# Two attentions and an mLSTM on one core: turned items copied before the next exponential, the first item inside the last dense block, the first decay weights beside the drain, heads' values one item later

## The chip, the cores and the metric

The kernel runs on one core of a Trainium2 chip. The metric is device time in microseconds (us) of one launch on that core; lower is better. TensorE (PE) multiplies, VectorE (DVE) and ScalarE (ACT) work on rows of 128 partitions, GpSimd (POOL) adds sums of squares, SyncE (SP) issues the weight transfers.

## What is computed

The reference runs two transformer blocks over one sequence of 512 tokens, width 1024, fp32. The change touches only the middle of the first block. Cut to that:

```python
h = rms_norm(x, mix_norm_pre)
(nq, kc, vc, ksl, vsl, kwn, vwn, gt, mq, mk, mv, mi, mf, mo) = split(h @ w_in)
o = native_sparse_attention(...)      # 8 heads of 64, compressed + selected + window branches, gated
hm = mlstm_chunkwise(mq, mk, mv, ...) # 4 heads, weights decay with distance, causal
y = concatenate([y_nsa, sigmoid(mo) * hm]) @ w_out
x = x + rms_norm(y, mix_norm_post)

h = rms_norm(x, xattn_norm_pre)
q = h @ w_xq;  k, v = split(rms_norm(mem) @ w_xkv)   # 4 heads of 256, 256 memory tokens
p = softmax(q k^T);  o = p v
x = x + rms_norm(o @ w_xo, xattn_norm_post)
```

Behind it come SwiGLU layers, a conformer convolution and a stick-breaking attention, which the change leaves as they are.

## The kernel before

Everything lives in SBUF; weights stream through a ring of four slots of 512 KB. A dense product splits weight and operand into a high and a low fp32r part and makes three products of them (`unit`, whose matmuls are all recorded at L515): one unit is 8 chunks x 3 products x 2 halves, 48 matmuls of 256 columns, and fills one PSUM bank. ACT makes the high part of each weight slot (`w_hi`, L1305), DVE the low part (`w_lo`, L1803). Each engine has its own program, written out by hand; they are held together by counting semaphores, so the order of the statements in each engine's loops is the order in which its instructions run. There are eight PSUM banks.

**The sparse attention** walks over 32 items, `NSA_ITEMS` = 4 column groups `c` x 4 query blocks `qb` x 2 branches. An item is 128 queries, two heads at once ("half"), and 128(qb+1) keys. Its steps:

1. PE: scores (`nsa_scores`, L854), into banks 0/1 or 2/3 by the item's parity; it waits until DVE has added item s-2.
2. DVE: adds the bias and finds the row maximum (`nsa_add`, L2159, two instructions).
3. ACT: exponential with row sum (L1466, two instructions).
4. DVE: reciprocal and scale (`nsa_scale`, L2166 and L2169).
5. PE: transposes the scaled item, "turns" it, into banks 4 and 5 (`nsa_turn`, L866). There is one pair of these banks, so it waits until ACT has copied the item before.
6. ACT: copies the turned item to `pT` (L1475).
7. PE: multiplies it with the values into bank 6 or 7 (`nsa_values`, L882); every eighth item adds the compressed branch (L888), and ACT and DVE take `h_hi` (L1483) and `h_lo` (L2149) out.

PE's round s does scores(s), turn(s-3), values(s-4). ACT's round s does exp(s), then copy(s-3). DVE's round s does add(s), scale(s-1). At items 8, 9, 16 and 17 (`NSA_SPLITS`) ACT and DVE also split one weight slot for the product with `w_out`. The first items stand behind the last `w_in` block, number 13, whose result DVE takes out (L1823); `in_values` transposes mLSTM values (L712) that DVE copies to `v_ml` (L1945), and `cmp_values_in` makes `v_cmp` (L2007, L2012).

**The mLSTM** follows: 8 items, each with scores (`ml_scores`, L902), decay weights by ACT (`ml_decays`, L1443/L1445), a product of the two by DVE (`ml_weight`, L2192), values (`ml_values`, L916), then column sums of one column each (L928, L935) and factors (L946).

**The cross attention** has 16 items, 4 heads x 4 query blocks, against 256 memory tokens: scores (L1051, banks 0 and 1), row maximum by DVE (L2310), exponential by ACT (L1532), reciprocal and scale by DVE (L2315, L2316), turn (L1061, banks 2 and 3), copy by ACT (L1542, two instructions of 128 columns), and after a head's fourth item its values (L1071, 8 slow matmuls in the trace's count), whose result ACT and DVE take out as `h_hi` (L1547) and `h_lo` (L2323). Then the product with `w_xo` follows (`dense_then_halves`).

## Time and profile before

| | |
|---|---|
| median of 3 runs | 2852.51 us (2851.51 to 2855.64) |
| the profiled execution's own time | 2848.28 us |
| its span in the trace | 2846.5 us |
| PE busy | 2768.2 us, 97% |
| DVE, ACT, POOL busy | 51%, 38%, 9% |

The profiled execution is 4.23 us below the median of the runs. PE is busy 97% of the span; the few places where it isn't are what a change of order can touch. A busy PE in this profile can still be a PE at half its clock.

### The profile page before, as it was taken

To read this page: it belongs to the slowest core of one execution; us is meant where nothing else is said; L and a number is where in the kernel's file an instruction comes from. 1 tells how busy PE (TensorE), PEld (TensorE's weight loads), DVE (VectorE), ACT (ScalarE), POOL (GpSimd) and SP (SyncE) were. 2 spreads that over 40 slices of the span, in tenths; PEclk is the share of its full clock that TensorE was granted. 3 is DMA by queue.
4 is the path that set the end of the run, shared out by engine and by line. 5 is a ranking of instruction groups with operands and counts; after the bars stand their busy time and mean duration, and the time that the engine had idled before them with its cause. 6 is when DMAs were issued, how large, how long until landed. Compare 5 with 4: busy or idle time off the path is not lost.

```text
span 2846.5 us, 56267 instructions
## 1 busy us (share of the span) xinstructions
PE 2768.2 (97%) x23426; PEld 2635.6 (93%) x23426; DVE 1454.3 (51%) x1911; ACT 1079.2 (38%) x1597; POOL 246.9 (9%) x211
## 2 busy tenths in 40 slices
PE   7988998999999999999999999999999999999997
PEld 7965996999999999997799999999999986999997
DVE  6766563554424544347865443335444367544433
ACT  4456433532324323236653232224343246422321
POOL 2000200100000000006810000000000000100000
PEclk9999999999999999999999999999999999999999
DMA  5310231223232332331122323343323332223232
GB/s 201 111 53 16 88 128 38 82 96 103 86 102 80 104 103 87 95 101 67 38 68 96 103 89 100 94 147 106 102 88 96 104 130 86 67 96 101 89 95 71
DMA packets 75161, 263.96 MB, mean 93 GB/s; under 512 B 8388, under 2 KB 8516, under 8 KB 74752
## 3 DMA queue, kind: packets, MB, share of 16 engines
q1 hardware_dynamic: 69408, 248.93, 27.0%
q10 hardware_dynamic: 4608, 8.39, 0.8%
q0 software_dynamic: 992, 4.42, 0.5%
q8 instruction: 118, 1.93, 0.3%
q14 instruction: 35, 0.29, 0.0%
HBM read 253.29 MB, written 8.42 MB: 92 GB/s over the span
## 4 chain that ended last, share of the span: by engine, by line
PE 92%; DVE 4%; ACT 2%; issue 2%; DMA 0%; SPq 0%; POOLq 0%; POOL 0%; DVEq 0%; ACTq 0%
PE bank L515 80%; PE bank L1089 2%; PE bank L568 1%; PE bank L632 1%; PE bank L1229 1%; DVE w_lo L1803 1%; PE bank L1071 1%; PE bank L1249 1%; PE bank L1261 0%; PE bank L866 0%; ACT w_hi L1305 0%; DVE n_p L2159 0%; ACT n_p L1466 0%; PE bank L916 0%; PE bank L854 0%
## 5 line engine op out<-in xcount | busy, mean ns | idle before, releaser
L515 PE MATMUL bank<-h_hi,w_hi 128*128 128x256 f32 x4720 | 931.2, 279 | 1.0 <-DVE w_lo L1803 0.7
L515 PE MATMUL bank<-h_hi,w_lo 128*128 128x256 f32 x4720 | 922.5, 277 | 0.0
L515 PE MATMUL bank<-h_lo,w_hi 128*128 128x256 f32 x4720 | 921.9, 277 | 0.0
L1803 DVE TENSOR_TENSOR w_lo<-w_raw,w_hi 128x1024 fp32r<-128x1024 f32 x468 | 577.3, 1237 | 376.0 <-ACT w_hi L1305 202.1
L515 PEld LDWEIGHTS bank<-h_hi,w_hi 128*128 128x128 f32 x4720 | 714.9, 188 | 11.7 <-issue 8.1
L515 PEld LDWEIGHTS bank<-h_hi,w_lo 128*128 128x128 f32 x4720 | 713.6, 188 | 0.0
L515 PEld LDWEIGHTS bank<-h_lo,w_hi 128*128 128x128 f32 x4720 | 713.0, 188 | 0.0
L1305 ACT ACTIVATE w_hi<-w_raw 128x1024 fp32r<-128x1024 f32 x468 | 476.9, 1050 | 230.2 <-PE bank L515 162.4
L1823 DVE TENSOR_TENSOR t<-bank,rB 128x512 f32<-128x512 f32 x260 | 179.2, 690 | 510.0 <-PE bank L515 507.1
L515 PE MATMUL bank<-a_hi,w_hi 128*128 128x256 f32 x1716 | 334.2, 276 | 0.0
L515 PE MATMUL bank<-a_lo,w_hi 128*128 128x256 f32 x1716 | 334.0, 276 | 0.0
L515 PE MATMUL bank<-a_hi,w_lo 128*128 128x256 f32 x1716 | 334.0, 276 | 0.0
L1345 ACT ACTIVATE a_hi<-t 128x512 f32 (+1 forms) x110 | 69.6, 632 | 581.2 <-DVE t L1861 581.2
L515 PEld LDWEIGHTS bank<-a_hi,w_hi 128*128 128x128 f32 x1716 | 258.4, 188 | 0.0
L515 PEld LDWEIGHTS bank<-a_lo,w_hi 128*128 128x128 f32 x1716 | 258.2, 188 | 0.0
L515 PEld LDWEIGHTS bank<-a_hi,w_lo 128*128 128x128 f32 x1716 | 258.2, 188 | 0.0
L2535 POOL TENSOR_TENSOR acc<-acc,sq 128x512 f32<-128x512 f32 (+1 forms) x72 | 94.6, 1314 | 1702.8 <-ACT sq L1311 1700.5
L1311 ACT ACTIVATE sq<-x 128x512 f32<-128x512 f32 (+1 forms) x56 | 35.3, 631 | 339.5 <-DVE x L1870 304.5
L1343 ACT ACTIVATE t<-t 128x512 f32<-128x512 f32 x110 | 69.7, 634 | 187.7 <-DVE t L1823 187.5
L1863 DVE TENSOR_TENSOR a_lo<-t,a_hi 128x512 f32 (+1 forms) x110 | 76.2, 693 | 100.6 <-ACT a_hi L1345 100.6
L1812 DVE SCALAR_TENSOR_TENSOR h_lo<-x,vec,h_hi 128x512 fp32r<-128x512 f32 (+1 forms) x64 | 71.0, 1125 | 66.5 <-ACT h_hi L1313 66.5
L2585 POOL TENSOR_TENSOR c_acc<-c_acc,c_product 128x512 f32<-128x512 f32 x63 | 87.9, 1395 | 9.8 <-ACT c_product L1622 5.0
(327 smaller groups left out, 2556.3 us busy)
## 6 DMA issues: line engine op xcount, KB each, us to landing
w_raw<-in_w_gu SPq DMA_DIRECT2D x220, 512.0 KB, 3.3
w_raw<-in_w_dn SPq DMA_DIRECT2D x80, 512.0 KB, 3.6
w_raw<-in_w_dn SPq DMA_DIRECT2D x40, 384.0 KB, 3.1
w_raw<-in_w_pw SPq DMA_DIRECT2D x24, 512.0 KB, 3.3
w_raw<-in_w_in SPq DMA_DIRECT2D x22, 512.0 KB, 4.5
w_raw<-in_w_xkv SPq DMA_DIRECT2D x16, 512.0 KB, 3.3
w_raw<-in_w_kv SPq DMA_DIRECT2D x16, 512.0 KB, 3.2
stick_qkv<-t ACTq DMA_DIRECT2D x24, 256.0 KB, 2.0
```

The costliest lines, as they stand in the source:

```text
L515: last = nc.tensor.matmul(dst[:, c:c + HALF], w, o[:, at + c:at + c + HALF], start=start and c == 0, stop=stop, skip_group_check=True)
L1089: last = nc.tensor.matmul(bank[4 + c % 2][:], diag_w[:, at:at + P], conv_tap(c, k), start=k == 0, stop=k == n - 1)
L1305: nc.scalar.activation(cut(w_hi, slot, UNIT), cut(w_raw, slot, UNIT), ACT.Copy).then_inc(w_hi_made, 1)
L1311: nc.scalar.activation(sq[:, (k % 2) * S:(k % 2) * S + n], cut(src, c, n), ACT.Square).then_inc(squared, 1)
L1343: nc.scalar.activation(t0[:], t0[:], ACT.Silu).then_inc(acted, 1)
L1345: nc.scalar.activation(cut(a_hi, c), t1[:], ACT.Copy).then_inc(f_hi, 1)
L1803: V.tensor_tensor(cut(w_lo, slot, UNIT), cut(w_raw, slot, UNIT), cut(w_hi, slot, UNIT).bitcast(f32), sub).then_inc(w_lo_made, 1)
L1812: V.scalar_tensor_tensor(cut(lo, c, n), cut(src, c, n), col(gain, c), hi_c, mult, sub).then_inc(op_lo, 1)
L1823: return V.tensor_tensor(dst, src, r, mult)
L1863: V.tensor_tensor(cut(a_lo, c), t1[:], cut(a_hi, c).bitcast(f32), sub).then_inc(f_lo, 1)
L2535: G.tensor_tensor(acc[:, 0:n], acc[:, 0:n], sq[:, (c % 2) * S:(c % 2) * S + n], add).then_inc(summed, 1)
L2585: G.tensor_tensor(acc_c, cut(c_product, (n - 1) % 4) if i == 1 else acc_c, cut(c_product, n % 4), add).then_inc(c_product_used, 2 if i == ...
```

## The change

- Sparse attention. `nsa_scores(0)` moves into the middle of dense unit 13 (after four of its eight chunks), and DVE does `cmp_values_in`, `nsa_add(0)` and `nsa_scale(0)` before it takes that unit's result out. `nsa_turn(0)` comes right behind `in_values(4)`, which gets bank 7 of its own.
- ACT copies the turned item s-3 first and does the exponential of item s after it.
- DVE splits its weight slots one item later.
- mLSTM: the first two score products move up among the last sparse items, ACT does the first three decays in its rounds 32, 33 and 34 (between the last copies), DVE does `ml_weight(0)`, `ml_weight(1)` and `ml_add(1)` before the last `h_lo`. The values go to banks 4 and 5 instead of 6 and 7, so they wait for the last copy of a turned item, not for the last `h_lo`.
- Cross attention: the first scores wait for six of eight `xq` results instead of all; turns come three items behind the scores instead of two (`px` has four slots instead of three); ACT copies first and with one instruction of 2x128 columns instead of two; a head's values come one item later; the last head's values stand inside the first two units of the product with `w_xo`.

```diff
-ML_COLUMN_BANK, FACTOR_BANK = [4, 5], [5, 4, 6, 7]
+ML_COLUMN_BANK, FACTOR_BANK = [6, 7], [7, 6, 4, 5]
...
+                    unit(r // RING, r % RING, in_bank(i), range(KC), h_hi, h_lo, True, True, made=R0["mix"] if r == 0 else None,
+                         within=(lambda: nsa_scores(0)) if n == 13 else None)
...
-                    pe.wait_ge(v_stored, 5)
+                    pe.wait_ge(v_stored, 3)
...
-                    pe.wait_ge(op_lo, R0["nsa"] + 4)
+                    pe.wait_ge(n_pT, NI + 1)
...
-            for s in range(NI + 4):
+            in_values(4)
+            nsa_turn(0)
+            for s in range(1, NI + 4):
                 if s < NI:
                     nsa_scores(s)
-                if s < 2:
-                    in_values(4 + s)
-                if 0 <= s - 3 < NI:
+                elif s < NI + 2:
+                    ml_scores(s - NI)
+                if s == 1:
+                    in_values(5)
+                if 1 <= s - 3 < NI:
                     nsa_turn(s - 3)
                 if s >= 4:
                     nsa_values(s - 4)
-                if NI < s < NI + 3:
-                    ml_scores(s - NI - 1)
...
-            for s in range(16 + 2):
+            for s in range(16 + 3):
                 if s < 16:
...
+                    x_scores(s)
+                r = s - 3
+                if r == 0:
+                    pe.wait_ge(evacuated, BEND["xq"])
                 if r >= 0:
...
+                    x_turn(r)
+                    if r and r % TB == 0:
+                        x_values(r // TB - 1)
+
+            for j in range(2):
+                pe.wait_ge(w_lo_made, U0["xo"] + j + 1)
+            xo_chunks(0, range(4))
+            x_values(3)
+            xo_chunks(0, (4, 5))
+            xo_chunks(1, range(6))
+            for j in range(2):
+                xo_chunks(j, (6, 7)).then_inc(w_used, 1)
+            dense_then_halves("xo", h_hi, h_lo, "post_x")
...
-                if s == NI + 3:
-                    ml_decays(0)
+                if NI <= s < NI + 3:
+                    ml_decays(s - NI)
...
+                if n == 13:
+
+                    cmp_values_in()
+                    nsa_add(0)
+                    nsa_scale(0)
                 dve.wait_ge(w_used, r + 1)
...
+            turn_in_values(4)
+            for s in range(1, NI + 6):
+                if s < NI:
+                    nsa_add(s)
+                if s == 1:
+                    turn_in_values(5)
+                if 1 <= s - 1 < NI:
+                    nsa_scale(s - 1)
+                if s - 1 in NSA_SPLITS:
+                    split("out", 0, 4, NSA_SPLITS.index(s - 1))
+                if s == NI + 2:
+                    ml_weight(0)
+                if s == NI + 3:
+                    ml_weight(1)
+
+                    dve.wait_ge(n_turned, NI - 1)
+                    ml_add(1)
```

What stands on PE behind the last `w_in` unit, before. L854 are scores of an item (`kS` and `kW` are its two branches' keys), L712 is `in_values`, L866 a turn of the item in `n_p`:

```order
L515 MATMUL bank0<-h_lo,w_hi 128x256 x2
L854 MATMUL bank0<-kS,qT 128x128 [waits evacuated] x2
L712 MATMUL bank1<-cst,t0 128x128 [waits v_stored,v_ready]
L712 MATMUL bank1<-cst,t0 128x128 x3
L854 MATMUL bank0<-kW,qT 128x128 [waits evacuated] x2
L712 MATMUL bank1<-cst,t1 128x128 [waits v_stored,v_ready]
L712 MATMUL bank1<-cst,t1 128x128 x3
L854 MATMUL bank0<-kS,qT 128x256 [waits nsa_add] x2
L854 MATMUL bank0<-kW,qT 128x256 [waits nsa_add] x2
L866 MATMUL bank1<-cst,n_p 128x128 [waits v_stored,nsa_scaled,cmp_out,nsa_pT]
L866 MATMUL bank1<-cst,n_p 128x128 [waits nsa_scaled]
L854 MATMUL bank0<-kS,qT 128x384 [waits nsa_add] x2
```

and of the change, from the same place (L516, L762, L715 and L871 are the same statements):

```order
L516 MATMUL bank0<-h_lo,w_hi 128x256 x2
L715 MATMUL bank1<-cst,t0 128x128 [waits ml_colout,v_stored,v_ready]
L715 MATMUL bank1<-cst,t0 128x128 x3
L871 MATMUL bank1<-cst,n_p 128x128 [waits v_stored,nsa_scaled,cmp_out,nsa_pT]
L871 MATMUL bank1<-cst,n_p 128x128 [waits nsa_scaled]
L762 MATMUL bank0<-kW,qT 128x128 [waits evacuated] x2
L715 MATMUL bank1<-cst,t1 128x128 [waits v_stored,v_ready]
L715 MATMUL bank1<-cst,t1 128x128 x3
L762 MATMUL bank0<-kS,qT 128x256 [waits nsa_add] x2
L762 MATMUL bank0<-kW,qT 128x256 [waits nsa_add] x2
L762 MATMUL bank0<-kS,qT 128x384 [waits nsa_add] x2
```

The turn of item 0 stood behind four score products and both `in_values`; now it stands behind one `in_values`, and item 0's scores are gone from here, up into unit 13.

What stands on ACT for the last items, before. L1466 is an exponential (x2: both halves), L1475 the copy of a turned item, L1443 and L1445 the decays, L1483 `h_hi`:

```order
L1466 ACTIVATE n_p,small<-n_p,small 128x512 [waits nsa_add] x2
L1475 ACTIVATE pT<-bank1 128x2x256 [waits nsa_pv,nsa_turned]
L1466 ACTIVATE n_p,small<-n_p,small 128x512 [waits nsa_add] x2
L1475 ACTIVATE pT<-bank1 128x2x384 [waits nsa_pv,nsa_turned] x2
L1475 ACTIVATE pT<-bank1 128x1024 [waits nsa_pv,nsa_turned] x2
L1443 ACTIVATE decay<-ml_space,ml_col 128x128 [waits ml_masked,ml_stab_in,ml_colout]
L1445 ACTIVATE decay<-ml_space,ml_col 128x384
```

and of the change (L1512 exponential, L1507 copy, L1481 and L1483 decays, L1521 `h_hi`):

```order
L1507 ACTIVATE pT<-bank1 128x2x256 [waits nsa_pv,nsa_turned]
L1512 ACTIVATE n_p,small<-n_p,small 128x512 [waits nsa_add] x2
L1507 ACTIVATE pT<-bank1 128x2x384 [waits nsa_pv,nsa_turned]
L1512 ACTIVATE n_p,small<-n_p,small 128x512 [waits nsa_add] x2
L1507 ACTIVATE pT<-bank1 128x2x384 [waits nsa_pv,nsa_turned]
L1481 ACTIVATE decay<-ml_space,ml_col 128x128 [waits ml_masked,ml_stab_in,ml_colout]
L1483 ACTIVATE decay<-ml_space,ml_col 128x384
L1481 ACTIVATE decay<-ml_space,ml_col 128x128
L1483 ACTIVATE decay<-ml_space,ml_col 128x384
L1507 ACTIVATE pT<-bank1 128x1024 [waits nsa_pv,nsa_turned]
```

The first copy of 2x384 columns, item 28's, stood behind the last exponential, item 31's; now it stands ahead of it. Four decay instructions now stand ahead of the copy of item 30.

What stands on PE at the end of the cross attention, before. L1061 is a turn, L1071 a head's values, L515 the first unit of the product with `w_xo`:

```order
L1061 MATMUL bank0<-cst,px 128x128 [waits x_pT,x_scaled]
L1061 MATMUL bank0<-cst,px 128x128
L1071 MATMUL bank1<-pxT,vx 128x512 [waits op_lo,x_pT]
L1071 MATMUL bank1<-pxT,vx 128x512
L1071 MATMUL bank1<-pxT,vx 128x512 [waits op_lo]
L1071 MATMUL bank1<-pxT,vx 128x512
L515 MATMUL bank0<-h_hi,w_hi 128x256 [waits op_lo,w_lo_made,evacuated]
```

and of the change, the last turn, the fourth chunk of unit 0, the last head's values and the fifth chunk (L1069 turn, L1080 values, L516 unit):

```order
L1069 MATMUL bank0<-cst,px 128x128 [waits x_pT,x_scaled]
L1069 MATMUL bank0<-cst,px 128x128
L516 MATMUL bank0<-h_hi,w_hi 128x256 [waits op_lo,w_lo_made]
...
L516 MATMUL bank0<-h_lo,w_hi 128x256 x2
L1080 MATMUL bank1<-pxT,vx 128x512 [waits op_lo,x_pT]
L1080 MATMUL bank1<-pxT,vx 128x512
L1080 MATMUL bank1<-pxT,vx 128x512 [waits op_lo]
L1080 MATMUL bank1<-pxT,vx 128x512
L516 MATMUL bank0<-h_hi,w_hi 128x256 [waits op_lo]
```

Half a unit of dense work now stands between the last turn and the values that need its copy.

## Rows read from the trace of the kernel before

**Rows 1.** The page: busy time by engine

```profile
PE 2768.2 (97%) x23426; PEld 2635.6 (93%) x23426; DVE 1454.3 (51%) x1911; ACT 1079.2 (38%) x1597; POOL 246.9 (9%) x211
```

**Rows 2.** Windows, both attentions whole: length, busy by engine, granted clock, DMA share, GB/s

```profile
165.95:265.94 99.99, 79.12 (x642) 46.84 (x641) 70.45 (x244) 66.44 (x179) 7.83 (x17) 0.97 0.10 33
442.22:484.43 42.21, 33.66 (x129) 20.50 (x129) 17.96 (x56) 18.59 (x71) 0.00 (x0) 1.00 0.00 0
```

**Rows 3.** PE's waits in the sparse attention: total, times, longest

```profile
PE bank L866 <- ACT pT L1475: 14.2, 15, 1.8
PE bank L866 <- DVE v_cmp L2012: 3.5, 1, 3.5
PE bank L916 <- DVE decay L2192: 2.6, 1, 2.6
```

**Rows 4.** Windows between the exponentials of items 7 and 15, 23 and 31, and behind

```profile
183.89:207.69 23.80, 18.38 (x159) 11.10 (x158) 18.06 (x60) 16.54 (x43) 3.63 (x8) 1.00 0.14 45
...
231.50:251.59 20.09, 18.21 (x159) 11.07 (x157) 14.66 (x58) 14.68 (x41) 0.00 (x0) 1.00 0.01 2
251.59:265.94 14.35, 10.55 (x105) 6.88 (x102) 4.63 (x12) 9.18 (x20) 0.00 (x0) 1.00 0.00 1
```

**Rows 5.** Timeline of one round, items 28 to 31: start, us, engine, line

```profile
249.70 1.13 PE L854 MATMUL bank<-kW,qT 64*128 64x512 f32 x4
251.27 0.87 PE L866 MATMUL bank<-cst,n_p 128*128 128x128 f32 x6 [0.44 <-ACT pT L1475]
251.59 0.72 ACT L1466 ACTIVATE n_p<-n_p,small 128x512 f32<-128x512 f32 x1 [0.38 <-DVE small L2159]
253.02 0.79 ACT L1475 ACTIVATE pT<-bank 128x768 f32<-128x768 f32 x1
253.86 0.88 PE L866 MATMUL bank<-cst,n_p 128*128 128x128 f32 x6 [1.13 <-ACT pT L1475]
```

**Rows 6.** Timeline of the start, items 0 to 4

```profile
172.05 1.13 DVE L2012 TENSOR_SCALAR v_cmp<-bank,of_group 128x128 f32<-128x128 f32 x4
173.28 0.66 PE L866 MATMUL bank<-cst,n_p 128*128 128x128 f32 x2 [3.49 <-DVE v_cmp L2012]
173.87 1.65 PE L854 MATMUL bank<-kS,qT 64*128 64x384 f32 x4
```

**Rows 7.** Windows of the start: DVE's stretch, and a stretch of low clock

```profile
166.06:183.15 17.09, 13.28 (x68) 6.37 (x68) 14.38 (x55) 9.13 (x32) 0.56 (x1) 0.80 0.18 63
173.00:179.00 6.00, 5.72 (x20) 2.60 (x20) 4.15 (x18) 2.95 (x11) 0.00 (x0) 0.50 0.01 3
```

**Rows 8.** Timeline at a split (item 8): ACT, DVE and PE

```profile
187.77 1.06 ACT L1305 ACTIVATE w_hi<-w_raw 128x1024 fp32r<-128x1024 f32 x1
188.86 1.23 DVE L1803 TENSOR_TENSOR w_lo<-w_raw,w_hi 128x1024 fp32r<-128x1024 f32 x1 [1.36 <-ACT w_hi L1305]
192.17 1.09 PE L866 MATMUL bank<-cst,n_p 128*128 128x128 f32 x8 [1.45 <-ACT pT L1475]
```

**Rows 9.** Timeline of ACT: first and last of the first item's four decays

```profile
260.58 0.39 ACT L1443 ACTIVATE decay<-ml_space,ml_col 128x128 f32<-128x128 f32 x1
261.67 0.60 ACT L1445 ACTIVATE decay<-ml_space,ml_col 128x384 f32<-128x384 f32 x1
```

**Rows 10.** PE's waits in the cross attention

```profile
PE bank L1071 <- ACT pxT L1542: 4.3, 4, 1.3
PE bank L1061 <- DVE px L2316: 3.2, 4, 1.5
PE bank L1051 <- DVE qx L1824: 0.8, 1, 0.8
```

**Rows 11.** Window from one head's values to the next head's

```profile
451.27:461.64 10.37, 8.42 (x32) 5.17 (x33) 4.40 (x14) 4.69 (x18) 0.00 (x0) 1.00 0.01 2
```

**Rows 12.** Critical chain: a head's values, and the first four units behind

```profile
481.29 3.70 PE bank L1071 x8
484.99 22.61 PE bank L515 x192
```

262 lines of the change are left out of this document (130 added, 132 removed).

## The prediction

> **What bounds the kernel now.** I read the page first, then the chain of waits over the whole span, then windows and the timeline where the change reaches. The page says PE is busy 97% of 2846.5 us [rows 1]: whatever the change gains must come out of PE's idle time, or out of time in which PE is busy at half its clock. The diff touches no stage outside two stretches. In the first, from the end of the last `w_in` unit to the first mLSTM values, PE is busy 79.12 of 99.99 us, in the second, the cross attention, 33.66 of 42.21 us [rows 2]. So 20.87 and 8.55 us are idle, 29.4 together. PE does no less work after the change, and everything behind it (the `w_out` product, `w_xo`, the layers) starts from results of these stretches, with weight transfers that use a tenth of the DMA engines there [rows 2]. I take it that each microsecond cut here comes off the end.
>
> The waits say what PE stood for. In the first stretch: 14.2 us in 15 waits for ACT's copy of a turned item, 3.5 us in one wait for `v_cmp` at the start, 2.6 us for the first decay weight [rows 3]; they make up 20.3 of the 20.87. In the second: 4.3 us before the four heads' values, 3.2 us before turns, 0.8 us for the last `qx` [rows 10].
>
> **The copy first.** Rows 5 show one round. Scores(31) end at 250.83; the exponential of item 31 starts at 251.59 on them, its two halves run until the copy of item 28 can start at 253.02; turn(29) starts at 253.86, 0.04 behind the copy's end, and PE stood 1.13 us. Turn(28), the only thing the copy truly needs, was over at 252.14. So ACT was held by an exponential that nobody needs for three rounds. Now the copy of item s-3 stands ahead of exponential s. Behind exponential(30) it could start at 252.2 and end at 253.0; PE has values(27) and the next scores in between, until about 252.7 here and later in a full round. The wait falls to 0.3 us or nothing.
>
> What limits a group of eight items then? PE's own work in it is 18.2 to 18.4 us. Between the exponentials of item 23 and item 31 (no split) it takes 20.09 us; between items 7 and 15, and again between 15 and 23 (23.81 us, the same in its rows), two weight slots are split, and it takes 23.80 [rows 4]. DVE is busy 18.06 of these with a split and 14.66 without, ACT 16.54 and 14.68: with a split DVE is as full as PE, and the two hand items to each other. So:
> - Two groups with splits: the floor is 18.4; I put 0.7 us on it for the handing over between two full engines, 19.1. Gain 2 x 4.7 = 9.4. A split costs ACT 1.06 and DVE 1.23 us, and the turn behind it waited 1.45 [rows 8]; DVE's part goes an item later, where no exponential waits for it.
> - The group without: floor 18.2, I take 18.6. Gain 1.5.
>
> **The start.** Before, DVE took out unit 13, then stored values, added items 0, 1 and 2, scaled, made `v_cmp` (1.13 us and a small reduction), and only then PE could turn item 0: an idle stretch of 3.49 us [rows 6]. Behind it PE worked at half clock: granted 0.50 from 173 to 179 us, that is 1.2 of 2.4 GHz, with 5.72 us busy, and the scores of 384 keys took 1.65 us [rows 6, 7]. What moves ahead of the unit's end has room there: the unit takes some 5.7 us of PE (four take 22.61 [rows 12]), DVE has little to do in it, and item 0 at 128 keys is small. Only its four score matmuls lengthen the unit, by what they took behind it. From 166.06 to the last add of the group, 183.15, DVE is busy 14.38 of 17.09 us: 2.7 idle, in waits for scores at half clock, and its busy part loses 1.4 us of `v_cmp` and some 1.2 us of item 0 [rows 6, 7]. Together 5.3; less 0.4 for the score matmuls and something for waits that stay, because the first rounds are a chain of small steps on three engines: gain 4.0 us until item 7. Bounds: nothing, if the chain stays as long; 6.4 us, if the 3.49 goes and with it the half clock (5.72 busy at 0.50 is 2.9 us too many).
>
> The Trainium skill, "TensorE: Matmul & The Clock Gate", Part 1, says the clock is throttled by default and busy time releases it, and that idle gaps between groups of matmuls make it swing. The trace agrees so far as the half clock from 173 us follows 3.49 us of idle [rows 6, 7]. If frequent small gaps did it too, the first rounds would stay slow, the start would gain 1 us instead of 4, and the sum below would be 21.5.
>
> **The drain.** From item 31's exponential to the first mLSTM values it is 14.35 us with 10.55 PE busy [rows 4]: the idle 3.8 are the 1.13 above and 2.6 for `ml_weight(0)`, which stood behind the last `h_lo`, behind `h_hi`, behind the last values. Now `ml_weight(0)` needs the first decays and scores, which are two rounds old. But the decays (four instructions, 260.58 to 262.27, 1.7 us [rows 9]) now stand before the copies of items 30 and 31. With scores(31) ending at t, turns and values of 0.8 to 1.0 us each, copies of 0.7 and 0.9, scores of 0.9 to 1.1 (about as in [rows 5, 8]): turn(28) to t+0.9, copy(28) 1.6, turn(29) 3.4, copy(29) 4.2, decays 5.9, turn(30) 6.1, copy(30) 7.1 (PE free at 6.9: 0.2 idle), second decays 8.6, turn(31) 8.1, copy(31) 9.5 (PE free at 9.1: 0.4 idle), last values with the compressed branch 11.5. Before it was 15.1. I take 3.0 of these 3.6. The new order has queued nothing else behind the decays: `h_hi` of the last group comes after them and feeds `h_lo`, needed only for the `w_out` product some 20 us on, and for the column sums, which now wait for it in place of the first values; they stand four value products later.
>
> **The cross attention.** Start: the first scores no longer wait for the last `qx`, gain 0.8 [rows 10]. One head takes 10.37 us from values to values, PE busy 8.42, of which the values are 3.70 [rows 11, 12]; four items' scores and turns are the rest, 1.18 each. The two idle pieces: 1.2 to 1.3 before the values, since they follow the turn at once and need its copy; 0.5 to 0.8 in the first round after them, since DVE and ACT stood through 3.70 us and `h_lo` then got in the way. The first goes (the copy has a round of 1.18 us, and takes 0.4). The second half stays: ACT now does `h_hi` (two of 0.6) between the copies of items two rounds later, and I work out 0.8 us of idle for the scores that need the next exponential. So 9.2 a head instead of 10.37, for the two whole heads 2.4. At the end: before, values(3) ended at 484.99 and two units behind it would end at 484.99 + 2 x 5.65 = 496.3 [rows 12]. After: first values at 451.0 (442.2, five items of 1.18, three scores more of some 0.87, 0.3 of waits) instead of 451.27 although two more items' scores and one more turn stand ahead of them (2.4 us of work done early); heads 9.2 apart; the third head's values end at 473.1; three turns 474.1; half a unit 476.9; values(3) 480.6; the other 12 chunks of the two units 8.5, 489.1. Gain 7.2 for the whole stretch; the last `h_hi`, `h_lo` (about 2.5 us) lie under 5.6 us of chunks. That leaves 1.35 of 8.55 us idle, which is tight; I take 6.6. Bounds: 0.8 and 8.55. `px` and the merged copy cost nothing: one copy of 256 columns instead of two of 128, on an ACT busy 18.59 of 42.21 us [rows 2].
>
> **The sum.** 4.0 + 9.4 + 1.5 + 3.0 + 6.6 = 24.5 us. The profiled execution's 2848.28 become 2823.8; the median of the runs lies 4.2 above it, so I forecast 2852.5 - 24.5 = 2828.0.
>
> **The rivals.**
> 1. *The forecast:* most of the idle goes. Gains of 17 to 32 us, 2820 to 2835.
> 2. *The waits change their place.* DVE and PE both need 18 us of each split group, and the first rounds are small steps. Were a split group to take 21 us instead of 19.1, the start gain 1 and the drain 1, and the heads' idle come back behind `h_hi`, x 3: 2 x 2.8 + 1 + 1 + 1 + 3 = 11.6, 2841. For it: busy DVE of 18.06 in 23.80 [rows 4]. Against: PE's waits name the copy 15 times and an add hardly ever [rows 3]. The clock belongs here: a stretch of 6 us at 0.50 costs 2.9 [rows 7], and one at a new place would take that from the gain.
> 3. *The change does not do what it says:* turns wait not for ACT's order but for turn, copy, turn as a chain. A turn of 768 columns and its copy take 0.88 + 0.79 [rows 5], PE has scores and values of 1.7 to 2.0 us beside them; only with equal times would all waits stay. Then only v_cmp, weights and the x start go: 3.5 + 2.6 + 0.8 = 6.9 less new waits: within 0.2%, 2847 to 2855.
> 4. *Slower.* ACT is strictly in order. The exponential of item s now waits for turn(s-3), which PE does after scores(s). If DVE then scales late and adds late, scores and turns come late: each of 28 rounds would grow by a turn and a copy less the slack, 1.7 us at 384 keys. It decides when exponential(s) ends later than DVE's scale slot, which stands behind add(s+1), one whole round of about 2.3 us after. Copy and exponential are 0.79 + 1.43 = 2.2 [rows 5]: nearly a round. Were it 0.5 us over in each of the 28 rounds, 14 us, the decays' 1.7 on the last copies with it, against 3.5 + 6.6 gained: +5 to +8, 2859. Against it: the scaled item is only needed by a turn two rounds later still.
>
> The skill, "PSUM — Partial Sum Buffer", section "Engine vs sequencer instructions", says that ScalarE's and VectorE's queues are strict FIFO; rows 5 agree (the copy stood 0.9 us behind the exponential with its own input ready). That rule is what both 1 and 4 hang on.
>
> **Chances.** 1: 0.72. 2: 0.17. 3: 0.07. 4: 0.04. Less than 0.2% (5.7 us) is about what a measurement of this kernel can't tell from no change. Faster 0.88, same 0.08, slower 0.04. Range: the floor is all idle and the half clock gone, 29.4 + 2.9 = 32.3, so 2820; the top is rival 2, 2842.
>
> **What would show it.** After: turn(0) within 1.5 us of the end of unit 13, no wait for `v_cmp`, granted clock 1.00 through the start; the exponentials of items 7, 15, 23 and 31 at distances of 19.1, 19.1 and 18.6 us; PE's waits for the copy of turned items 14.2 -> under 4 us; no wait for the first decay weight; waits before a head's values gone, some 0.8 us for scores instead. If instead PE waits for adds or scales of DVE in the split groups, rival 2; if the copies still end last, rival 3; if exponentials start behind copies and DVE waits for them, rival 4. Wrong by another way: an extra stretch at half clock in the mLSTM's one-column sums, which the trace has already and whose place may shift.

## The result, and the profile after

The changed kernel takes 2820.79 us (median of 4 runs, 2815.65 to 2824.83) against 2852.01 us for the kernel before (4 runs beside it, 2851.0 to 2855.64): a ratio of 0.9887, 95% interval 0.9869 to 0.9906. That is 31.2 us less. The forecast was 24.5 us less, 2828.0, in a range of 2820 to 2842. The median lies 0.8 us above the low end of that range, and two of its four runs (2815.65 and 2819.87) lie below it. The direction and the places were right, the sum was 6.7 us too small. The profiled execution took 2815.65 us, its span is 2813.9 instead of 2846.5 us, 32.6 less.

The page's first line of the kernel after, which answers to [rows 1]:

```profile
PE 2761.1 (98%) x23426; PEld 2633.6 (94%) x23426; DVE 1454.2 (52%) x1911; ACT 1076.9 (38%) x1581; POOL 247.3 (9%) x211
```

PE makes the same 23426 matmuls. ACT has 16 instructions fewer, the merged copies of the cross attention. Windows of the kernel after (start and end, length, then busy us by engine, granted clock, DMA share, GB/s): the sparse attention whole, its three groups of eight items, the drain, the 6 us that ran at 0.50 before, one head of the cross attention, from values to values, and two places of low clock in the mLSTM behind:

```profile
166.60:244.49 77.89, 75.52 (x641) 46.03 (x639) 68.36 (x231) 65.21 (x175) 7.82 (x17) 1.00 0.12 42
179.80:198.36 18.56, 18.21 (x157) 11.15 (x158) 17.87 (x60) 16.41 (x44) 3.62 (x8) 1.00 0.18 58
198.36:216.87 18.51, 18.12 (x157) 11.05 (x158) 17.81 (x60) 16.36 (x43) 3.64 (x8) 1.00 0.17 58
216.87:234.83 17.96, 17.70 (x154) 10.89 (x156) 14.54 (x58) 14.69 (x41) 0.00 (x0) 1.00 0.01 2
234.83:244.49 9.66, 9.19 (x90) 5.92 (x88) 5.82 (x11) 8.38 (x20) 0.00 (x0) 1.00 0.01 3
...
173.00:179.00 6.00, 6.00 (x44) 3.09 (x44) 5.89 (x22) 5.39 (x17) 0.00 (x0) 1.00 0.01 3
426.85:435.37 8.52, 8.17 (x33) 5.30 (x33) 4.49 (x15) 4.28 (x14) 0.00 (x0) 1.00 0.01 2
...
256.00:259.00 3.00, 3.00 (x6) 1.58 (x7) 2.23 (x7) 0.30 (x1) 0.00 (x0) 0.50 0.00 0
273.00:276.00 3.00, 3.00 (x17) 3.00 (x16) 0.20 (x1) 0.18 (x1) 0.00 (x0) 0.50 0.00 0
```

In the sparse attention PE was idle 20.87 of 99.99 us [rows 2] and is now idle 2.37 of 77.89. A group with two split slots went from 23.80 to 18.56 and 18.51, the one without from 20.09 to 17.96, the drain from 14.35 to 9.66 [rows 4], a head from 10.37 [rows 11] to 8.52. The start runs at full clock where it had 0.50 [rows 7].

PE's waits after, in the sparse attention and then in the cross attention (total us, times, longest; L871 is the turn, L1060 the scores, L1069 the turn of the cross attention):

```profile
PE bank L871 <- ACT pT L1507: 0.8, 3, 0.3
PE bank L715 <- DVE v_ml L1983: 0.4, 1, 0.4
PE bank L762 <- DVE small L2108: 0.2, 1, 0.2
...
PE bank L1060 <- ACT px L1579: 1.0, 3, 0.4
PE bank L1069 <- ACT pxT L1574: 0.3, 1, 0.3
```

Against [rows 3, 10]: the copy's 14.2 us in 15 waits are 0.8 in 3, the waits for `v_cmp` and for the first decay weight are gone, and of the cross attention's 4.3 + 3.2 + 0.8 us there remain 1.3, two of them the 0.35 before scores that the forecast named. In the sparse attention DVE ends a wait of PE only twice, 0.6 us in all, and PE's values wait once more for the copy, 0.2 us. DVE did not become the bound, although it is busy 17.87 of 18.56 us.

The timeline of the drain after, ACT's part and the first mLSTM values on PE (start, us, engine, line):

```profile
234.13 0.81 ACT L1507 ACTIVATE pT<-bank 128x768 f32<-128x768 f32 x1
...
234.83 0.71 ACT L1512 ACTIVATE n_p<-n_p,small 128x512 f32<-128x512 f32 x1
...
236.58 0.81 ACT L1507 ACTIVATE pT<-bank 128x768 f32<-128x768 f32 x1 [0.23 <-PE bank L871]
...
237.28 0.39 ACT L1481 ACTIVATE decay<-ml_space,ml_col 128x128 f32<-128x128 f32 x1
...
239.08 1.22 DVE L2219 SCALAR_TENSOR_TENSOR decay<-bank,decay 128x1024 f32<-128x1024 f32 x1 [1.50 <-ACT decay L1483]
...
239.25 1.02 ACT L1507 ACTIVATE pT<-bank 128x1024 f32<-128x1024 f32 x1 [0.28 <-PE bank L871]
...
240.33 1.09 PE L871 MATMUL bank<-cst,n_p 128*128 128x128 f32 x8 [0.31 <-ACT pT L1507]
...
244.49 0.70 PE L921 MATMUL bank<-decay,v_ml 128*128 128x512 f32 x1
```

The copy of item 28 starts at 234.13, ahead of item 31's exponential and as soon as its turn is over; before, it stood behind both halves of that exponential and started 0.9 us after its turn was over [rows 5]. The first decay weight is started at 239.08 and done at 240.30, 4.2 us before PE asks for it; the decays ahead of the copies cost PE two short waits, 0.31 us before turn(31) and 0.17 us before its values.

**Where the 32.6 us of the two profiles went.** Event times of the traces, the kernel before and the kernel after; "T" is the start of the product of `cmp_w` and `cmp_h` just ahead of unit 13 (159.48 and 160.00), the last thing on PE that both kernels have alike:

| stretch | before | after | gain | forecast |
|---|---|---|---|---|
| start: T to item 7's exponential | 24.41 | 19.80 | 4.6 | 4.0 |
| items 7 to 15, 15 to 23 | 23.80, 23.81 | 18.56, 18.51 | 10.5 | 9.4 |
| items 23 to 31 | 20.09 | 17.96 | 2.1 | 1.5 |
| drain: to the first mLSTM values | 14.35 | 9.66 | 4.7 | 3.0 |
| to the first scores of the cross attention, without the wait for `qx` | 176.28 | 173.17 | 3.1 | 0 |
| cross attention to the end of its first four `w_xo` units, that wait counted | 65.22 | 56.66 | 8.6 | 6.6 |
| up to T, and all layers behind | | | -1.0 | 0 |

These marks are ACT's, and the change moves ACT's exponentials against PE: item 31's starts 2.67 us behind the start of its scores where it was 1.89. PE's own marks, the starts of scores(7), (15), (23) and (31), give each part its own gain. The windows before, from T to the first mLSTM values:

```profile
159.48:181.99 22.51, 18.73 (x145) 12.42 (x144) 14.41 (x54) 7.97 (x28) 0.56 (x1) 0.85 0.13 48
181.99:205.53 23.54, 18.34 (x159) 11.06 (x157) 17.79 (x60) 16.33 (x44) 3.17 (x7) 1.00 0.14 46
205.53:229.33 23.80, 18.33 (x159) 11.05 (x157) 17.98 (x60) 16.47 (x44) 3.64 (x8) 1.00 0.14 45
229.33:249.70 20.37, 18.20 (x159) 11.05 (x157) 15.03 (x58) 14.97 (x42) 0.45 (x1) 1.00 0.01 2
249.70:265.94 16.24, 12.00 (x111) 7.50 (x109) 6.39 (x19) 10.70 (x25) 0.00 (x0) 1.00 0.00 1
```

and after:

```profile
160.00:176.84 16.84, 15.95 (x145) 11.63 (x144) 13.16 (x51) 7.58 (x28) 0.56 (x1) 1.00 0.18 64
176.84:195.30 18.46, 18.13 (x159) 11.06 (x157) 17.77 (x61) 16.76 (x44) 3.17 (x7) 1.00 0.18 58
195.30:213.80 18.50, 18.12 (x158) 11.05 (x156) 17.80 (x61) 16.34 (x44) 3.64 (x8) 1.00 0.17 58
213.80:232.16 18.36, 18.06 (x159) 11.06 (x157) 14.94 (x59) 14.69 (x42) 0.46 (x1) 1.00 0.00 1
232.16:244.49 12.33, 11.86 (x110) 7.49 (x108) 8.45 (x20) 10.72 (x25) 0.00 (x0) 1.00 0.01 4
```

By these the start gained 5.7 us (forecast 4.0), the two split groups 10.4 (9.4), the group without 2.0 (1.5) and the drain 3.9 (3.0).

### The profile page after: what moved, and what is told of

The parts are those of the page before. It is cut to its first block, busy times and chain, and to the rows that moved or that the text cites. A ratio compares the mean times of both kernels' runs of the same rounds, so it can differ in the third digit from the quotient of the medians.

```text
span 2813.9 us, 56255 instructions
## 1 busy us (share of the span) xinstructions
PE 2761.1 (98%) x23426; PEld 2633.6 (94%) x23426; DVE 1454.2 (52%) x1911; ACT 1076.9 (38%) x1581; POOL 247.3 (9%) x211
## 4 chain that ended last, share of the span: by engine, by line
PE 93%; DVE 3%; ACT 2%; issue 1%; DMA 0%; SPq 0%; POOLq 0%; POOL 0%; DVEq 0%; ACTq 0%
PE bank L516 81%; PE bank L1127 2%; PE bank L569 1%; PE bank L633 1%; PE bank L1267 1%; PE bank L762 1%; PE bank L1287 1%; PE bank L871 1%; PE bank L1299 0%; PE bank L1080 0%; PE bank L887 0%; DVE w_lo L1841 0%; PE bank L921 0%; PE bank L1060 0%; DMA cst<-in_consts 0%
## 5 line engine op out<-in xcount | busy, mean ns | idle before, releaser
L516 PE MATMUL bank<-h_hi,w_hi 128*128 128x256 f32 x4720 | 931.1, 279 | 1.1 <-DVE w_lo L1841 0.8
L516 PE MATMUL bank<-h_hi,w_lo 128*128 128x256 f32 x4720 | 922.2, 277 | 0.0
L516 PE MATMUL bank<-h_lo,w_hi 128*128 128x256 f32 x4720 | 921.9, 277 | 0.0
L516 PEld LDWEIGHTS bank<-h_hi,w_hi 128*128 128x128 f32 x4720 | 714.6, 188 | 11.9 <-issue 8.1
L516 PEld LDWEIGHTS bank<-h_hi,w_lo 128*128 128x128 f32 x4720 | 713.2, 188 | 0.0
L516 PEld LDWEIGHTS bank<-h_lo,w_hi 128*128 128x128 f32 x4720 | 712.8, 188 | 0.0
L516 PE MATMUL bank<-a_lo,w_hi 128*128 128x256 f32 x1716 | 334.2, 276 | 0.0
L516 PE MATMUL bank<-a_hi,w_hi 128*128 128x256 f32 x1716 | 334.1, 276 | 0.0
L516 PE MATMUL bank<-a_hi,w_lo 128*128 128x256 f32 x1716 | 334.0, 276 | 0.0
L516 PEld LDWEIGHTS bank<-a_lo,w_hi 128*128 128x128 f32 x1716 | 258.4, 188 | 0.0
L516 PEld LDWEIGHTS bank<-a_hi,w_hi 128*128 128x128 f32 x1716 | 258.3, 188 | 0.0
L516 PEld LDWEIGHTS bank<-a_hi,w_lo 128*128 128x128 f32 x1716 | 258.2, 188 | 0.0
```

What stands on the lines that cost most here:

```text
L516: last = nc.tensor.matmul(dst[:, c:c + HALF], w, o[:, at + c:at + c + HALF], start=start and c == 0, stop=stop, skip_group_check=True)
```

## The experiments

Ten kernels, in the order in which they ran. Two lengths are used throughout, since each lies between two events of one trace and the rest of the span doesn't touch it: **T to mLSTM**, from T above to the first mLSTM values (106.46 before, 84.49 after), and **the cross stretch**, from its first scores to the end of the first four `w_xo` units (64.44 and 56.66). Where a gain is given from medians, the runs of one kernel scatter by 2 to 9 us, and by 24 in the 19 runs of the kernel before that stood beside the first four experiments.

### The copy first, alone

In the kernel before, ACT's loop copies item s-3 ahead of exponential s, and nothing else changes:

```diff
             for s in range(NI + 5):
-                if s < NI:
-                    for half in range(2):
-                        act.wait_ge(n_add, 2 * s + half + 1)
...
                 r = s - 3
...
                     nc.scalar.activation(dst, banks[1][:, 0:2 * S].rearrange("p (h n) -> p h n", n=S)[:, :, 0:n], ACT.Copy).then_inc(n_pT, 1)
+                if s < NI:
+                    for half in range(2):
+                        act.wait_ge(n_add, 2 * s + half + 1)
...
```

> The kernel before with one edit: in the sparse attention's loop ACT copies the turned item s-3 first and does exponential s after it. Theory A (the exponential held the copy): most of the 14.2 us in 15 waits for the copy goes; items 7, 15, 23, 31 stand some 20, 20 and 18.6 us apart instead of 23.8, 23.8 and 20.1; the kernel gains 9 to 13 us (ratio 0.9955 to 0.997). Theory B (turn, copy, turn is the chain, or DVE binds): the waits stay or change to waits for scores and adds; it gains under 3 us.

Measured: 2838.64 us against 2853.57, ratio 0.9936 (0.9916 to 0.9956). A split group and the group without a split:

```profile
184.59:204.00 19.41, 18.44 (x161) 11.22 (x160) 17.22 (x57) 16.56 (x44) 3.58 (x8) 1.00 0.16 55
223.45:241.41 17.96, 17.55 (x152) 10.66 (x152) 14.54 (x58) 14.70 (x41) 0.00 (x0) 1.00 0.01 2
```

PE's waits for the copy fell from 14.2 us in 15 to 3.0 us in 8; those for `v_cmp` (3.5) and the decay (2.6) stayed. T to mLSTM is 94.53, 11.9 us less by one exchange in one loop. The median fell by 14.9 us, more than the 9 to 13 named; the 11.9 of the trace is within them. The group without a split has its whole gain by this; the split groups have 4.4 of their 5.3. That the copy stood behind an exponential that nobody needed yet is shown: nothing else was moved.

### The cross attention, alone

The kernel before with the cross attention of the change only: first scores ahead of the last `qx`, four `px`, one copy of both halves, turns a round later, values an item later, the last head's values inside the two first units.

```diff
-            for s in range(16 + 2):
+            for s in range(16 + 3):
...
-                r = s - 2
+                r = s - 3
...
+                    x_turn(r)
+                    if r and r % TB == 0:
+                        x_values(r // TB - 1)
...
+            xo_chunks(0, range(4))
+            x_values(3)
+            xo_chunks(0, (4, 5))
+            xo_chunks(1, range(6))
```

> The kernel before with the cross attention's part of the change alone (scores before the last qx, turns three items behind, copy first and in one instruction, values an item later, last head's values inside the first two units). Theory A (the two parts are independent): from the end of xq to the end of the first four xo units it takes the 56.7 us that the whole change shows, against 65.4 before, so 8.7 us less, and the kernel gains 8 to 9 us (ratio 0.997). Theory B (part of that gain comes from the earlier stretches or from the clock): under 6 us.

Measured: 2842.62 us, ratio 0.9955 (0.9936 to 0.9975). The cross stretch is 56.68, the same as in the whole change, so the two parts of the change don't act on one another. The profiled T to mLSTM was 108.15 here, 1.7 more than in the kernel before with the same instructions: items 15 to 23 took 25.40 us at a granted clock of 0.93, not 23.81 at 1.00. That was the first sign that the half clock has its own part in these lengths.

### Without the start

The changed kernel with the start of before: item 0's scores not in unit 13, `v_cmp` and `in_values` back behind it.

```diff
-                         within=(lambda: nsa_scores(0)) if n == 13 else None)
...
-            in_values(4)
-            nsa_turn(0)
-            for s in range(1, NI + 4):
+            for s in range(NI + 4):
```

> The changed kernel with the start put back: item 0's scores, add and scale and v_cmp behind the last w_in unit, turn(0) in round 3. Theory A: PE idles 3 to 3.5 us before turn(0) again and falls to half clock behind it; 6 to 7 us slower than the changed kernel (item 7's exponential again 17 to 18 us behind the unit's end). Theory B (the copy order alone would have shortened the start): 3 us or less slower.

Measured: 2825.35 us, ratio 0.9893 (0.9854 to 0.9931), 4.6 above the changed kernel by the medians, whose runs overlap, and under the 6 to 7 that were expected. T to mLSTM is 89.85, 5.4 more; T to item 7's exponential 25.20 instead of 19.80. The wait for `v_cmp` of 3.5 us is back, and behind it the half clock (a window of this kernel; the kernel after has 1.00 from 173 to 179 us):

```profile
175.00:180.00 5.00, 5.00 (x20) 2.01 (x18) 3.16 (x13) 2.48 (x10) 0.00 (x0) 0.50 0.01 3
```

### The exponential first, in the changed kernel

```diff
             for s in range(NI + 5):
+                if s < NI:
+                    for half in range(2):
+                        act.wait_ge(n_add, 2 * s + half + 1)
...
                 r = s - 3
...
-                if s < NI:
-                    for half in range(2):
-                        act.wait_ge(n_add, 2 * s + half + 1)
...
```

> The changed kernel with ACT's order in the sparse attention put back: exponential s first, copy s-3 after it. Theory A: the waits for the copy are back, some 9 to 13 us slower than the changed kernel, 18 to 23 us faster than before. Theory B (the start and the later split on DVE did most of it): under 5 us slower.

Measured: 2831.45 us, ratio 0.9916 (0.9883 to 0.9948), 10.7 above the changed kernel; T to mLSTM is 92.73, 8.2 more. PE's waits for the copy are 8.7 us in 14. The groups:

```profile
177.92:198.36 20.44, 18.15 (x158) 10.95 (x157) 18.00 (x60) 16.42 (x43) 3.63 (x8) 1.00 0.15 53
218.80:238.89 20.09, 18.21 (x159) 11.07 (x158) 14.65 (x58) 14.68 (x41) 0.00 (x0) 1.00 0.01 2
```

The group without a split is the 20.09 of before to the hundredth, which is the copy's 2.1 us. But a group with splits takes 20.44, not 23.80: 3.4 us of each are gone without the copy. One edit was left that reaches DVE in these groups, DVE's part of the split an item later, and the next kernel has it alone.

### DVE's part of a split an item later, alone

In the kernel before:

```diff
-                if s in NSA_SPLITS:
-                    split("out", 0, 4, NSA_SPLITS.index(s))
+                if s - 1 in NSA_SPLITS:
+                    split("out", 0, 4, NSA_SPLITS.index(s - 1))
```

> The kernel before with one edit: DVE splits its weight slot of items 8, 9, 16, 17 one item later (behind the next item's add and scale). ACT's exponential still stands ahead of the copy. Theory A (from the run with the exponential first, whose split groups took 20.4 us): the later split alone brings the groups between items 7, 15 and 23 from 23.8 to 20.4 us each and leaves the third at 20.1. Theory B (it only helped together with the earlier start): over 22.5 us each.

Measured: one run, 2842.87 us; T to mLSTM 99.01. The first split group and the group without:

```profile
184.35:204.77 20.42, 17.84 (x155) 10.72 (x154) 17.99 (x60) 16.40 (x43) 3.62 (x8) 1.00 0.17 53
225.20:245.29 20.09, 18.22 (x159) 11.09 (x158) 14.67 (x58) 14.67 (x41) 0.00 (x0) 1.00 0.01 2
```

So the one line gives 3.4 us a split group, the exchange on ACT 4.4 (above), both together 5.3: they shorten the same wait from two sides. A reading that fits all three kernels, and the timeline of before at item 8's split:

```profile
190.00 0.28 DVE L2159 CUSTOM_DVE_ANT_0 n_p<-bank,toep 128x128 f32<-128x128 f32 x1
190.33 0.40 ACT L1466 ACTIVATE n_p<-n_p,small 128x128 f32<-128x128 f32 x1 [1.50 <-DVE small L2159]
```

DVE stood 1.36 us for `w_hi` and made `w_lo` until 190.0 [rows 8], with item s+1's add behind it; then that item's exponential came late (ACT stood 1.50 us for the add), behind it ACT's copy (191.12), and behind that the turn (192.17, PE stood 1.45 us). Take the copy out from behind the exponential, and a late add hardly reaches PE; take the split out from before the add, and the exponential is on time.

### Without the drain

The changed kernel with decays, first weights and mLSTM scores where they stood before.

```diff
-                if NI <= s < NI + 3:
-                    ml_decays(s - NI)
+                if s == NI + 3:
+                    ml_decays(0)
...
-                if s == NI + 2:
-                    ml_weight(0)
-                if s == NI + 3:
-                    ml_weight(1)
```

> The changed kernel with the drain's order put back (mLSTM scores, decays 0 to 2, weights 0 and 1 and the first sum behind the sparse items; the banks stay as changed). Theory A: PE waits 2.6 us for the first weight again, and from item 31's exponential to the first mLSTM values it takes some 12.3 us instead of 9.66. Theory B (the wait moves into the mLSTM phase anyway, the early weights only move it): the distance grows, but from item 31 to the first w_out unit the kernel is under 1 us longer.

Measured: one run, 2826.49 us. T to mLSTM 87.41, 2.9 more than in the changed kernel, and in the waits stands the old line:

```profile
PE bank L921 <- DVE decay L2219: 2.6, 1, 2.6
```

From item 31's exponential to the first values it is 12.56 us here, 9.66 in the changed kernel and 14.35 before. The drain's edits together are worth 2.9, and the other 1.8 us come with the copy: the kernel with the copy first alone also has 12.56. Some 0.8 of these 1.8 are the shift of ACT's mark. Theory B falls as well: from scores(31) to the first `w_out` unit it is 39.35 us here and 33.22 in the changed kernel, and with the loss to the half clock taken off (5.1 and 1.7 us: length times what the granted clock is short of 1.00) 34.2 and 31.5. The 2.7 us don't come back in the mLSTM.

### A head's values right behind its last turn

In the changed kernel:

```diff
-                    if r and r % TB == 0:
-                        x_values(r // TB - 1)
+                    if r % TB == 3 and r < 15:
+                        x_values(r // TB)
```

> The changed kernel with a head's values (heads 0 to 2) right behind the turn of its fourth item instead of one item later; all else of the cross attention as changed. Theory A: PE waits for the copy before three heads' values, 0.6 to 1.2 us each: the stretch from the first scores to the end of four xo units takes 58.5 to 60 us instead of 56.7. Theory B (the gain of this stretch is in the other edits): under 1 us more.

Measured: one run, 2819.48 us; the cross stretch 58.74 instead of 56.66. PE's waits there:

```profile
PE bank L1080 <- ACT pxT L1574: 1.7, 3, 0.6
PE bank L1069 <- DVE px L2363: 0.9, 2, 0.5
PE bank L1060 <- ACT px L1579: 0.3, 1, 0.3
```

Three waits for the turned item are back, 1.7 us in all. Taken out of the whole, the values an item later cost 2.1 of the 8.6 us of the cross attention; the time of this one run, 2819.48, is within the scatter of the changed kernel's and shows nothing of it. The early first scores take away a wait of 0.8 us. The rest, 5.7 us, comes from the turns an item later, the copy ahead of the exponential, the merged copy and the last head's values within the units; how these share it was not tried.

### Wide matmuls between the one-column sums

The first table has 3.1 us of gain between the first mLSTM values and the cross attention, where PE has the same instructions in both kernels. PE is busy 98% of that stretch, and the traces show parts of it at 0.50. Ahead of the first such part in the kernel after, PE made the one-column sums (L935, L942) from 252.56 to 256.43, 32 matmuls of one column each:

```profile
254.37 2.20 PE L942 MATMUL bank<-cst,sq_ml 128*128 128x1 f32 x16
```

Such a matmul counts as busy time like any other, though it feeds one column. The experiment adds 16 matmuls of 256 columns between these sums, extra work, whose results nothing reads:

```diff
+            def wide(pair):
+                nc.tensor.matmul(bank[ML_COLUMN_BANK[pair]][:, HALF:2 * HALF], h_hi[:, 0:P], h_hi[:, 0:HALF], start=False, stop=True,
...
+                        if k % 2:
+                            wide(pair)
```

> The changed kernel with 16 matmuls of 256 fp32r columns more, into columns of the bank that nobody reads, one for every two of the mLSTM's one-column sums; each costs 0.1 to 0.2 us of PE, 2 to 3 us together. Theory A (PE falls to half clock because these sums leave its array nearly unused): granted clock 1.00 through the mLSTM and the first w_out units; the stretch from the first mLSTM values to the xkv stage, 77.96 us at a clock of 0.96, becomes no longer, or up to 1 us shorter, despite the added work. Theory B (the half clock comes from elsewhere): the stretches at 0.50 stay and it is 2 to 3 us longer.

Measured: 2822.27 us, ratio 0.9898 (0.9882 to 0.9915), not distinguishable from the changed kernel. The stretch is 177.97 us at 0.96, 2.4 more than the 175.61 at 0.96 of the changed kernel's second execution (below), so the added work costs about what theory B named. Windows of this kernel, the whole stretch and two places in it:

```profile
241.06:419.03 177.97, 176.11 (x1373) 163.72 (x1372) 101.45 (x141) 66.63 (x103) 21.80 (x20) 0.96 0.29 95
253.00:256.00 3.00, 3.00 (x14) 2.85 (x14) 0.38 (x3) 0.00 (x0) 0.00 (x0) 0.50 0.00 0
271.00:274.00 3.00, 3.00 (x21) 3.00 (x21) 1.04 (x6) 0.30 (x1) 0.00 (x0) 0.70 0.00 0
```

The half clock is still there, so theory A fell in the form in which it was put: sixteen wide matmuls don't remove it. That the sums have nothing to do with it does not follow. In the first block five wide matmuls and 18 of the 32 sums had been started when the clock fell, at 251.75.

The traces speak for the sums. Each has two blocks of 32 of them. In the twelve profiles the clock fell 22 times between the first mLSTM values and the cross attention after 4 us in which PE was never idle; each of these 22 falls stands inside such a block or at most 1.4 us behind its end, and 22 of the 24 blocks have one. The other falls of that stretch all follow idle time of PE. So the sums are the likely cause; no run without them was made, and it is not shown.

### Both kernels once more

Both kernels again, with a comment line added, to see how far one execution differs from the next. They ran on another chip than the eight experiments above.

> The kernel before, unchanged but for a comment line, profiled a second time. Question: is the microseconds' gain behind the first attention (first mLSTM values to first scores of the cross attention, 177.06 us before, 173.17 us after, with the same instructions) the change's, or does the place and length of the half-clock stretches differ from one execution to the next of one kernel? Theory A (executions differ): the distances between the exponentials of items 7, 15, 23 and 31 repeat within 0.1 us (23.80, 23.81, 20.09), but the 177.06 us come out different by 1 to 4 us, and the granted clock of 0.50 stands at other times than 278 to 282 and 292 to 298 us. Theory B (the change's order sets it): 177.06 within 0.5 us, and the half clock at the same times. Span 2841 to 2848 by A, 2846.5 by B.

> The changed kernel, unchanged but for a comment line, profiled a second time. Theory A (executions differ in where the half clock falls): distances between the exponentials repeat within 0.1 us (18.56, 18.51, 17.96), the 173.17 us from the first mLSTM values to the first scores of the cross attention come out different by 1 to 4 us (172 to 177), with the 0.50 at other times than 256 to 259 and 273 to 277 us. Theory B (the order sets it): 173.17 within 0.5 us. Span 2813 to 2819 by A, 2813.9 by B.

Measured: spans 2850.2 and 2814.3 us. The kernel before again, a split group, the stretch from the mLSTM's first values to the cross attention, and the cross stretch:

```profile
184.50:208.28 23.78, 17.92 (x155) 10.72 (x154) 18.03 (x60) 16.52 (x43) 3.62 (x8) 1.00 0.14 45
266.51:443.04 176.53, 173.89 (x1354) 159.98 (x1354) 102.93 (x142) 66.65 (x105) 21.76 (x20) 0.96 0.29 96
443.04:509.17 66.13, 58.35 (x320) 43.86 (x321) 23.06 (x60) 26.48 (x82) 3.89 (x3) 0.97 0.09 29
```

and the kernel after again:

```profile
176.87:195.43 18.56, 18.22 (x157) 11.15 (x158) 17.86 (x60) 16.41 (x44) 3.62 (x8) 1.00 0.17 58
...
241.56:417.17 175.61, 173.75 (x1356) 160.79 (x1355) 101.29 (x141) 66.63 (x103) 21.76 (x20) 0.96 0.29 97
417.17:473.85 56.68, 55.25 (x323) 43.60 (x321) 24.26 (x61) 24.91 (x66) 4.39 (x3) 1.00 0.11 33
```

Where the clock is 1.00, distances that are bound by the order of the engines repeat to 0.03 us: 23.78, 23.79 and 20.09; 18.56, 18.51 and 17.96; T to mLSTM 84.48. The stretch behind doesn't: 173.17 and 175.61 us for the changed kernel, 177.06 and 176.53 for the one before, which with its wait of 0.78 us for `qx` taken off is 176.28 and 175.75. By the second pair the gain there is 0.1 us, not 3.1. The two executions of the changed kernel fell to half clock behind the same sums, 95.9 and 112.9 us behind T in the first and 95.4 and 112.5 in the second, but the second stayed there twice as long, 6.8 and not 3.4 us each time. The first of the two places in the kernel after, and below it in its second execution:

```profile
255.90:259.20 3.30, 3.30 (x8) 1.68 (x7) 2.43 (x7) 0.30 (x1) 0.00 (x0) 0.50 0.00 0
...
252.50:259.25 6.75, 6.75 (x17) 3.56 (x17) 3.16 (x9) 0.30 (x1) 0.00 (x0) 0.50 0.00 0
```

Theory A holds for the changed kernel in the lengths, but the place in the program is nearly the same. For the kernel before the 176.53 miss the 1 to 4 us by which they were to differ, and the span of 2850.2 the 2841 to 2848; there it was the cross stretch, 1.7 us longer at a clock of 0.97 and not 1.00, and the start, at T to exponential 7 of 23.71 and not 24.41, with a clock of 0.93 and not 0.86.

## What held of the prediction, and the step that failed

**The step that failed** is the size of the terms, all five in the same direction: 24.5 us forecast, 30.5 measured. The two largest misses are the cross attention, put at 6.6 and measured at 8.6, and the start, put at 4.0 and measured at 5.7 by PE's marks. Its range failed with them: its low end, 2820, took all idle time and the half clock of the start as the most that could go and the rest of the kernel as fixed, while the rest moved by 2 us in the first pair of profiles.

**The mechanism** held step by step. Turn(0) starts at 167.36, 0.3 us behind the end of unit 13 (167.08); no wait for `v_cmp`; the clock is 1.00 through the start; the copy's waits are 0.8 us where under 4 were named; no wait for the decay weight; 0.35 us for scores, where 0.8 was named, in place of the waits before a head's values. Of the rivals, "the waits change their place" fell with PE's two short waits for DVE in the sparse attention, "the change does not do what it says" with the 11.9 us of the copy alone, and "slower" with 17.96 us for 8 items, 2.25 a round: copy and exponential, 2.2, fit. ScalarE's strict order, taken from the Trainium skill, "PSUM — Partial Sum Buffer", section "Engine vs sequencer instructions", is what the exchange used, and the traces agree: the copy of item 28 had its input at 252.14 and started at 253.02, behind the exponential [rows 5], and with the same instructions in another order the stretch is 11.9 us shorter.

**The sizes.** Worked out by the same steps, by ACT's marks as in the forecast:

- *Split groups, 9.4 forecast, 10.5 measured.* Too large was "the floor is 18.4; I put 0.7 us on it for the handing over between two full engines". The hand-over is 0.35 and 0.39 us (18.56 less 18.21, 18.51 less 18.12), and the floor 0.2 to 0.3 below the 18.4. DVE's part of the split was named and priced with nothing of its own; alone it gives 3.4 us a group.
- *The group without, 1.5 and 2.1 (2.0 by PE's marks).* The 18.2 us of busy time were nearly a floor: the same 156 matmuls (x159 in the rows, with those that reach over the ends of the window) are busy 18.20 us before and 18.06 after. PE's idle time beside them is 0.30 us where 0.4 was put. ACT's marks mislead here. Their window is busy 18.21 us before and 17.70 after, but it holds 43 matmuls of turns before and 40 after. The 0.1 to 0.2 us by which busy time does shrink come from the records' ends, which run past the start of the next matmul: a head's values are recorded at 3.70 us [rows 12] behind a wait and at 3.60 in a stream, and in the stream the next scores start 3.44 us after theirs (426.68 to 430.12). The Trainium skill, "TensorE: Matmul & The Clock Gate", Part 2, "Single matmul latency", puts the drain of a matmul at about 175 ns. The 0.16 us between 3.60 and 3.44 lies near it, but ends of matmuls are modelled in this profile, so it is no measurement of the drain.
- *The drain, 3.0 and 4.7.* The schedule step by step was right: by it the first values come 11.5 us behind the end of scores(31), and that end, 233.29, to 244.49 is 11.2. It gave 3.6, of which the forecast took 3.0; measured in this way it is 15.1 - 11.2 = 3.9. The rest is a shift of the marker: exponential 31 now starts some 1.5 us behind the end of its scores and not 0.8, so some 0.8 us of the 4.7 belong to what came before it.
- *The start, 4.0 and 4.6* by exponential 7, whose marker has shifted in the same way; by PE's marks it is 5.7, and by taking the start out 5.4. That is near the bound of 6.4 (the wait and the half clock both gone), since little of the chain of small steps was left: PE is idle 0.89 of 16.84 us. The half clock of before also lasted 6.8 us and not the 6 of the window that was read, and its length is luck: in the second execution of the kernel before this stretch is 0.7 us shorter. The sentence of the Trainium skill that was weighed there ("TensorE: Matmul & The Clock Gate", Part 1: idle gaps between groups of matmuls make the clock swing) would have made it 1 us; gaps of up to 0.45 us did nothing to the clock here.
- *The cross attention, 6.6 and 8.6.* "I work out 0.8 us of idle for the scores" was 0.35, and the values cost 3.44 and not 3.70: heads are 8.52 apart and not 9.2. That is 1.4 us over the two whole heads, and the worked-out 7.2 had been cut to 6.6 for being tight. It wasn't.
- *Behind, 0 forecast, 3.1 in the first pair of profiles and 0.1 in the second.* It was named at the end of the forecast as a way to be wrong, with no number. Whether any of it is the change's is open. In the six profiles in which PE waits 2.6 us for the first decay weight, the half clock costs this stretch 6.8 us five times and 8.5 once; in the six without that wait 3.4 three times and 6.8 three times. In five of the first six the clock also falls right behind that wait, and in none of the others. Twelve profiles are too few to settle it.

The terms as measured, 4.6 + 10.5 + 2.1 + 4.7 + 8.6, are 30.5 us against 24.5, and the medians differ by 31.2. About half of the 6.0 us is one habit: a term was worked out and then an allowance for waits not seen was put on it, 0.7 a split group, 0.4 for the group without, 0.6 in the drain, 0.6 in the cross attention and some 0.9 at the start. In the groups 0.35, 0.39 and 0.30 us of it came, elsewhere none. The other half is in the working itself: the heads 0.7 us too long each, the first rounds of the start, and marks that shift. Written out instruction by instruction, the drain was within 0.3 us, but the cross attention was 1.4 off, so writing it out is no guarantee.

## What to carry to other kernels

On an engine that works strictly in order, put what the bound engine waits for ahead of what is only needed rounds later: one exchange of two blocks in ACT's loop gave 11.9 us of PE's 20.9 idle. When such a stall is sized, write out the rounds with durations from the timeline and keep the result, and take both ends of a measured stretch from the bound engine: by ACT's exponentials the start gained 4.6 us and the drain 4.7, by PE's scores 5.7 and 3.9. And edits on one chain don't add: alone they gave 3.4 and 4.4 us, together 5.3, so each is tried alone and taken out alone before it is given a price.

## What was not expected of the hardware

PE's clock fell to half in a stretch in which the profile calls it busy nearly throughout. The last two windows of the kernel after, in the first fence of windows above, show it: 0.50 at 256 to 259 and 273 to 276 us, with PE busy 3.00 of 3.00 in both. But ahead of each fall PE made one-column sums, from 252.56 and from 268.21 on, and this holds for all 22 such falls of the twelve profiles, as told with the experiment on wide matmuls. The Trainium skill, "TensorE: Matmul & The Clock Gate", Part 1, "What's actually happening", says that how many matmuls run before the clock rises varies from run to run. Here a stretch at half clock behind the same sums lasted 3.4 us in one execution and 6.8 in the next. The same section says that activity releases the throttle. By these rows a busy share in the profile is not what the clock follows. Adding up length times what the granted clock is short of 1.00, the stretch from the first mLSTM values to the cross attention lost 3.4 us in three of twelve profiles, 6.8 in eight and 8.5 in one. That the sums set it off is likely and not shown. A difference of 2 to 3 us between single profiles of this kernel says nothing unless the clock of the stretch is shown beside it.
